# Setting up a token mixer: diagonals on VectorE, stores awaited later, first rows loaded early, a convolution moved into other tiles

## The chip, the cores and the metric

One Trainium2 chip, one of its cores. The metric is the device time of one execution in microseconds; lower is better. The kernel before was timed in three executions (5937.07, 5937.58 and 5954.27 us), of which the median, 5937.58 us, is the figure to be predicted against. One more execution was taken with the profiler.

## The reference

The program computes one layer of a decoder for a prompt of 2048 tokens and eight samples of eight tokens. The change touches two of its three token mixers, which both read the input projection `z`:

```python
z = h @ w_in
o_rw, wkv_T, shift_T = rwkv7_mix(z[..., :896], shift0, wkv0, ...)        # recurrence over tokens, 4 heads of 64
o_cv, conv_T = conformer_conv_mix(z[..., 896:1408], conv0, ...)

# rwkv7_mix:           zs = z + (z_prev - z) * mu_shift ; ... ; returns z[:, -1] as shift_T
# conformer_conv_mix:  u = z_a * sigmoid(z_b)
#                      u_pad = concat([conv0, u])               # 30 earlier rows per sequence
#                      c = causal_dwconv(u_pad, conv_w) + conv_b # 31 taps, each channel by itself
#                      return silu(layernorm(c)), u_pad[:, -30:]
```

`shift_T` (the last row of `z` of the prompt and of each sample) and `conv_T` (the last 30 rows of `u`) are outputs of the program.

## The kernel before, in words

The program runs phases one after the other: the input projection, the recurrent mixer `rwkv` with the convolution, the convolution's layer norm (`conv_finish`), attention of the prompt and of the samples, the output projection, and the gated MLP in two phases. Within a phase the five engines run their own instruction lists, written out by hand, and meet at semaphores; a `Block` ends with a barrier of all engines.

`rwkv` has two such blocks.

**The setup block** (L1204). SP issues, in this order, the loads for the convolution (weights, biases, `z`, the samples' earlier rows; `conv_inputs.sync`), the mixer's parameters (L1220, L1223), eight stores of last rows of `z` from DRAM to DRAM, four bytes a piece (`shift_p` L1225, seven times `shift_s` L1227), waits until the parameters and the eight stores have landed, then waits for ScalarE's last copy of the convolution's state, stores it (three stores, L2035 and L2036) and waits for these too (L2038). GpSimd makes masks and constants (L1246 to L1277), then the 62 diagonal matrices `cv["diag"]` (128 x 128, identity times one column of weights; two blocks of channels by 31 taps, L1281). ScalarE takes sigmoids, VectorE the products `u` into `cv["up"]` (prompt) and `cv["us"]` (samples), TensorE and ScalarE transpose the state.

**The main block** (L1283). SP loads the rows of `z` for a tile of 128 tokens into `zin` (two DMAs of 128 x 7 x 65 numbers, L1289): tile 0 on entry, tile i+1 or later when an earlier tile's shifted rows `zs` are made. TensorE first computes the samples' convolution: 62 products (block, tap) of a diagonal with `cv["us"]`, 64 columns each, into bank 4 of PSUM (L1546); it signals `conv_made`, ScalarE copies the two halves out (L1691) and signals `conv_taken`. Only then does TensorE go on to `keys_and_lora(main, 0)` and the 16 tiles of the prompt. A float32 product is two passes in the trace. Each prompt tile has 62 products of the prompt's convolution spread into places where TensorE would wait for another engine (`conv(n)` in `body`: 2, 4, 2, 6, 5, 5, 4, 4 and the rest at the end). Then follow four tiles of two samples each, whose `body` has no such products. `front` (VectorE, ScalarE) prepares the first tile: differences of rows `zd`, shifted rows `zs`, squares of keys `sqk`; ScalarE's `low_rows` needs `zs`, and TensorE's `keys_and_lora` needs `sqk` and `low_rows`. In `body` VectorE prepares the next tile's rows first (`shift`).

GpSimd has nothing to do in the main block until the prompt's last state is made.

Of the kernel before, what the change touches and what calls it, by code (L numbers as in the profile page):

```python
# [1066 lines left out]
def rwkv(nc, ident, t, cv):  # L1067
# [8 lines left out]
    with ExitStack() as ctx:  # L1076
# [123 lines left out]

        conv_made, conv_taken = [ctx.enter_context(nc.semaphore("rw_" + x)) for x in ("sample_conv_made", "sample_conv_taken")]

        setup = nc.Block()
        with ExitStack() as conv_ctx, setup:  # L1204
# [5 lines left out]
            @setup.sync  # L1210
            def _(sp):
                conv["sync"](sp)
                with nc.allow_non_contiguous_dma(reason="parameters by channel"):
                    loads = ((mu[:, :], t["mu_shift"].rearrange("(b p) -> p b", p=P)), (w0[:, :], t["w0"].partition_broadcast(P)),
                             (chp[:, 0, :], t["a0"].rearrange("(b p) -> p b", p=P)), (chp[:, 1, :], t["k_k"].rearrange("(b p) -> p b", p=P)),
                             (chp[:, 2, :], t["k_a"].rearrange("(b p) -> p b", p=P)), (ln_g[:, :], t["lnx_g"].partition_broadcast(P)),
                             (ln_b[:, :], t["lnx_b"].partition_broadcast(P)), (lora[0:32, :], t["w_lora"]), (lora[32:64, :], t["a_lora"]),
                             (lora[64:128, :], t["g_lora"]))
                    for dst, src in loads:
                        sp.dma_start(dst, src).then_inc(par, 16)  # L1220
                    sp.wait_ge(const, 1)
                    for h in range(H):
                        sp.dma_start(rk_w[64 * (h % 2):64 * (h % 2) + 64, h // 2, h:h + 1], t["r_k"][h, :].unsqueeze(1)).then_inc(par, 16)  # L1223

                    sp.dma_start(t["shift_p"].rearrange("o (b p) -> b p o", p=P), t["zT"][0:7, :, SEQ:SEQ + 1]).then_inc(shift_st, 16)  # L1225
                    for b in range(7):
                        sp.dma_start(t["shift_s"][:, b * P:(b + 1) * P].rearrange("j p -> p j"),  # L1227
                                     t["zT"][b, :, SEQ + 1:NT + 1].rearrange("p (j s) -> p j s", s=DEC_SEQ)[:, :, DEC_SEQ - 1]).then_inc(shift_st, 16)
                sp.wait_ge(par, 16 * (len(loads) + H))
                sp.wait_ge(shift_st, 16 * 8)  # L1230
                conv["sync_last"](sp)

            @setup.gpsimd
            def _(pool):
# [42 lines left out]
                own(pool.tensor_tensor(cmask[:, 1:2], sel8[:, 0:1], sel8[:, 1:2], ALU.add))  # L1277
                pool.wait_ge(conv["parameters"], 16 * 5)
                for b in range(CONV_B):
                    for j in range(CONV_W):  # L1280
                        pool.tensor_scalar(cv["diag"][:, b, j, :], ident, cv["w"][:, b, j:j + 1], None, ALU.mult)  # L1281

# [3 lines left out]
        def _(sp):  # L1286
# [6 lines left out]

            load(0)
            sp.wait_ge(*main["vec"].at("zs", 0))
# [24 lines left out]
        @block.gpsimd  # L1320
        def _(pool):
            pool.wait_ge(wkv_made, 1)
            for hp in range(2):
                pool.dma_start(t["wkv_p"].rearrange("(b two) v k -> two v b k", two=2)[hp], S_out[64 * hp:64 * hp + 64, 0, :, :]).then_inc(wkv_st, 16)
            with pool.Fori(0, S_TILES) as i:
# [6 lines left out]
                for c in range(2):  # L1332
                    pool.dma_start(t["oT"][0:2, :, bass.ds(i * 16 + (SEQ + c * DEC_SEQ), DEC_SEQ)].rearrange("b p t -> p b t"),
                                   oT_sb[:, :, c * C:c * C + DEC_SEQ]).then_inc(samp["o"].sem, 16)
            pool.wait_ge(wkv_st, 32)
            pool.wait_ge(*main["o"].at("o", TILES - 1))
# [11 lines left out]
        def _(pe):  # L1348
# [28 lines left out]

            def body(g, i, behind, ahead):
                s = g["pe"]
# [8 lines left out]

                taps = iter(() if g["sample"] else [(b, j) for b in range(CONV_B) for j in range(CONV_W)])

                def conv(n):

                    mm = None
                    for b, j in itertools.islice(taps, n):
                        mm = mul(bank(4)[:, b * P:(b + 1) * P], cv["diag"][:, b, j, :], cv["up"][:, b, bass.ds(i * P + j, P)], j == 0, j == CONV_W - 1)
                    return mm
# [143 lines left out]
                mm = conv(CONV_B * CONV_W)  # L1540
                if mm is not None:
                    mm.then_inc(*s.step("conv"))

            for b in range(CONV_B):
                for j in range(CONV_W):
                    mm = pe.matmul(bank(4)[:, b * TS:(b + 1) * TS].rearrange("p (s t) -> p s t", t=DEC_SEQ), cv["diag"][:, b, j, :], cv["us"][:, b, :, j:j + DEC_SEQ],  # L1546
                                   start=j == 0, stop=j == CONV_W - 1, skip_group_check=True)
            mm.then_inc(conv_made, 1)
            pe.wait_ge(conv_taken, 1)
            keys_and_lora(main, 0)  # L1550
# [13 lines left out]
            pe.wait_ge(*main["vec"].at("out", TILES - 1))  # L1564
            pe.wait_ge(*main["act"].at("oT", TILES - 1))
            keys_and_lora(samp, 0)
            decays(samp, 0)
            body(samp, 0, False, True)
            with pe.Fori(1, S_TILES - 1) as i:
                body(samp, i, True, True)  # L1570
            body(samp, S_TILES - 1, True, False)
            turn_out(samp, S_TILES - 1)

        @block.scalar
        def _(act):
# [112 lines left out]

            act.wait_ge(conv_made, 1)
            for b in range(CONV_B):  # L1690
                op = act.activation(cv["c"][:, b, SEQ:NT], bank(4)[:, b * TS:(b + 1) * TS], ACT.Identity, bias=cv["par"][:, 0, b:b + 1])  # L1691
            op.then_inc(conv_taken, 1)
            act.activation(warm[:, :], eps[:, :], ACT.Sigmoid)
# [302 lines left out]
def conv_inputs(nc, ident, t, cv, ps_t, ctx):  # L1996
# [15 lines left out]
    st_ld = ctx.enter_context(nc.semaphore("cv_state_loaded"))  # L2012
    stored = ctx.enter_context(nc.semaphore("cv_state_stored"))
    pe_s = Steps(nc, ctx, "cv_in_pe", ["in0", "in1", "out0", "out1", "out2"])
# [58 lines left out]

    def vector(dve):
        for b in range(CB):
            dve.wait_ge(*act_s.at(f"sig{b}", 0))
# [8 lines left out]

    return dict(sync=sync, sync_last=sync_last, gpsimd=gpsimd, tensor=tensor, scalar=scalar, vector=vector, parameters=par_ld)

# [1426 lines left out]
```

## Time and profile before

| | |
|---|---|
| median of three executions | 5937.58 us |
| the profiled execution: time | 5945.43 us |
| the profiled execution: span from first to last instruction | 5943.8 us |
| TensorE busy in the span | 4890.8 us (82%) |
| VectorE busy | 2526.8 us (43%) |
| ScalarE busy | 1904.2 us (32%) |
| GpSimd busy | 305.0 us (5%) |
| mean granted TensorE clock | 0.848 of full speed |

The profiled execution's span is within 1.7 us of its own time; that time is 7.9 us above the median of the three. In rows of a timeline the columns are: start in us, length in us of the group, engine (PE is TensorE, PEld its weight loads, DVE VectorE, ACT ScalarE, POOL GpSimd, SP SyncE, a q behind the name its queue), line, operation, what is written and read, shape, how many, and in brackets the idle time before and what ended it. In the windows view each row is a stretch, with each engine's busy us and number of instructions, then the granted clock of TensorE (1.00 is full speed), the busy share of the DMA engines and GB/s.

### The profile page before, as it was taken

The page shows a single profiled execution, that of the slowest core. Times are in us where ns is not written, and L with a number is a line of the kernel's source. Part 1 is how long each engine was busy: PE and PEld are TensorE (multiplying, and loading weights), DVE is VectorE, ACT ScalarE, POOL GpSimd, SP SyncE. Part 2 cuts the span into 40 slices and gives each one's busy share as a digit, 9 for nine tenths or more (in the row PEclk, how much of TensorE's full clock was granted, in tenths as well). Part 3 has the DMA queues.
Part 4 walks back from the last instruction along what each step waited for, and adds up shares of the span by engine and source line. Part 5 has one row for each costly group of instructions (what it writes and reads, how often), then busy time and mean ns, then how long its engine had stood idle before and what let it go on. Part 6 is the DMA issues. An engine that isn't in the chain of part 4 may idle for free. (4 is left out here: it accounts for less than half of the span.)

```text
span 5943.8 us, 68433 instructions
## 1 busy us (share of the span) xinstructions
PE 4890.8 (82%) x25340; PEld 3691.2 (62%) x25340; DVE 2526.8 (43%) x5235; ACT 1904.2 (32%) x3217; POOL 305.0 (5%) x473
## 2 busy tenths in 40 slices
PE   8999499998734566777776448888999999899999
PEld 4444388887612344545555135677888888787877
DVE  1111056765546776777861453323222222212133
ACT  1000033333326665666764432222111111101043
POOL 0000300000000000000001000010000000000000
PEclk9999589998855555666788768899999999999999
DMA  3110300000020000000002013443111111434321
GB/s 132 49 49 36 48 14 13 15 15 7 7 71 17 13 13 7 13 7 3 5 3 90 18 45 126 141 149 95 43 43 43 43 43 43 153 120 151 106 70 59
DMA packets 316997, 315.02 MB, mean 53 GB/s; under 512 B 145115, under 2 KB 266425, under 8 KB 310409
## 3 DMA queue, kind: packets, MB, share of 16 engines
q1 hardware_dynamic: 286713, 175.80, 11.0%
q0 software_dynamic: 30096, 136.76, 6.3%
q8 instruction: 112, 1.84, 0.1%
q14 instruction: 76, 0.62, 0.0%
HBM read 211.29 MB, written 102.33 MB: 53 GB/s over the span
## 5 line engine op out<-in xcount | busy, mean ns | idle before, releaser
L639 PE MATMUL fu_ps<-fu_h_hi,fu_w_lo 128*128 128x512 f32 (+1 forms) x1760 | 654.3, 372 | 34.9 <-DVE fu_h_lo L696 30.1
L640 PE MATMUL fu_ps<-fu_h_lo,fu_w_hi 128*128 128x512 f32 (+1 forms) x1760 | 653.5, 371 | 0.0
L641 PE MATMUL fu_ps<-fu_h_hi,fu_w_hi 128*128 128x512 f32 (+1 forms) x1760 | 652.2, 371 | 0.0
L2510 PE MATMUL ap_ps<-ap_V,ap_PT 128*128 128x64 f32 x2176 | 412.6, 355 | 216.7 <-ACT ap_PT L2635 216.1
L2510 PEld LDWEIGHTS ap_ps<-ap_V,ap_PT 128*128 128x128 f32 x2176 | 379.2, 263 | 270.7 <-ACT ap_PT L2635 270.6
L879 PE MATMUL fd_ps<-fd_w_lo,fd_a_hi 128*128 128x512 f32 (+1 forms) x1088 | 428.6, 394 | 21.5 <-DVE fd_w_lo L1010 18.1
L880 PE MATMUL fd_ps<-fd_w_hi,fd_a_lo 128*128 128x512 f32 (+1 forms) x1088 | 426.4, 392 | 0.0
L881 PE MATMUL fd_ps<-fd_w_hi,fd_a_hi 128*128 128x512 f32 (+1 forms) x1088 | 426.2, 392 | 0.0
L639 PEld LDWEIGHTS fu_ps<-fu_h_hi,fu_w_lo 128*128 128x128 f32 x1760 | 336.7, 191 | 93.8 <-issue 35.8
L640 PEld LDWEIGHTS fu_ps<-fu_h_lo,fu_w_hi 128*128 128x128 f32 x1760 | 336.6, 191 | 56.4
L641 PEld LDWEIGHTS fu_ps<-fu_h_hi,fu_w_hi 128*128 128x128 f32 x1760 | 336.2, 191 | 56.6
L271 PE MATMUL pi_psz<-pi_hT,pi_w 128*128 128x512 f32 (+1 forms) x880 | 341.0, 559 | 5.4 <-ACT pi_hT L236 5.4
L2531 PE MATMUL ap_ps<-ident,ap_lg 128*128 128x128 f32 x1088 | 223.9, 354 | 124.2 <-ACT ap_lg L2606 109.6
L2719 DVE TENSOR_SCALAR_CACHE_REDUCE ap_seen<-ap_sc,ap_srch 128x384 bf16<-128x384 f32 (+13 forms) x210 | 310.1, 1477 | 5.3
L2531 PEld LDWEIGHTS ap_ps<-ident,ap_lg 128*128 128x128 f32 x1088 | 174.0, 192 | 208.2 <-ACT ap_lg L2606 153.1
L2613 ACT ACTIVATE ap_sgn<-ap_sc,ap_srch 128x384 bf16<-128x384 f32 (+13 forms) x224 | 292.4, 1305 | 2.9
L672 ACT ACTIVATE fu_gpre<-fu_ps 128x512 f32<-128x512 f32 x88 | 52.5, 599 | 723.3 <-PE fu_ps L641 723.3
L271 PEld LDWEIGHTS pi_psz<-pi_hT,pi_w 128*128 128x128 f32 x880 | 171.5, 219 | 172.6 <-issue 171.7
L277 PE MATMUL pi_psz<-pi_w,pi_hT 128*128 128x512 f32 (+3 forms) x816 | 266.1, 489 | 0.0
L710 DVE TENSOR_SCALAR fu_gate<-fu_gpre,fu_cw 128x2048 f32<-128x2048 f32 x22 | 29.6, 1347 | 537.9 <-ACT fu_gprs L672 487.5
L1353 PE MATMUL rw_ps<-cv_up,cv_diag 128*128 (+1 forms) x1984 | 245.5, 276 | 0.0
L879 PEld LDWEIGHTS fd_ps<-fd_w_lo,fd_a_hi 128*128 128x128 f32 (+1 forms) x1088 | 202.5, 186 | 68.1 <-issue 18.1
(514 smaller groups left out, 8212.6 us busy)
## 6 DMA issues: line engine op xcount, KB each, us to landing
fd_x<-x SPq DMA_DIRECT2D x48, 512.0 KB, 4.6
aT<-fu_gate POOLq DMA_DIRECT2D x22, 1056.0 KB, 8.0
fu_w_raw<-in_ffn_up SPq DMA_DIRECT2D x44, 512.0 KB, 5.4
fd_a<-aT SPq DMA_DIRECT2D x32, 704.0 KB, 5.0
x<-fd_x POOLq DMA_DIRECT2D x32, 512.0 KB, 3.0
zT<-pi_zc POOLq DMA_DIRECT2D x44, 256.0 KB, 2.3
fd_w_raw<-in_ffn_down SPq DMA_DIRECT2D x10, 1024.0 KB, 11.7
za<-pi_za POOLq DMA_DIRECT2D x16, 546.0 KB, 3.2
```

What stands on the lines that cost most here:

```text
L271: mm = pe.matmul(psz[:, bank, 0:n_tok], w[:, k, c * P:(c + 1) * P], hT[:, k, 0:n_tok], start=(k == 0), stop=(k == KD - 1))
L277: mm = pe.matmul(psz[0:n, bank, 0:m], hT[:, k, s * P:s * P + n], w[:, k, N_CM + at:N_CM + at + m], start=(k == 0), stop=(k == KD - 1))
L639: pe.matmul(out, wl, hh, start=(k == 0), stop=False)
L640: pe.matmul(out, wh, hl, start=False, stop=False)
L641: mm = pe.matmul(out, wh, hh, start=False, stop=(k == KD - 1))
L879: pe.matmul(out, a_hi[:, s, k, 0:n], w_lo[:, k, cols], start=first, stop=False)
L880: pe.matmul(out, a_lo[:, s, k, 0:n], w_hi[:, k, cols], start=False, stop=False)
L881: return pe.matmul(out, a_hi[:, s, k, 0:n], w_hi[:, k, cols], start=False, stop=last)
L2510: return pe.matmul(out, lhsT, rhs, start=start, stop=stop, skip_group_check=True)
L2531: mm = pe.transpose(pb[4 + b][:, x * P:(x + 1) * P], lg[:, h, k * P:(k + 1) * P], ident)
L2613: act.activation(sgn[:, 0:keys(g)], sc[:, g % 3, 0:keys(g)], ACT.Sign, bias=state[:, NCAND:NCAND + 1], accum_out=s2[:, 0:1]).then_inc(*act ...
L2719: dve.tensor_scalar(seen[:, 0:keys(i)], row, col(CAND), 0.0, ALU.is_ge, ALU.add, accum_out=got).then_inc(*vec_s.step(f"t{i}_{r}"))
```

## The change

Five edits in `rwkv` and `conv_inputs`:

1. The 62 diagonals are made by VectorE, ahead of its products `u`, once the convolution's parameters are loaded (`conv_inputs.vector`).
2. The eight `shift` stores move from SP's setup to the start of GpSimd's list in the main block; the waits for them and for the three stores of the convolution's state move to the end of that list.
3. SP loads the first tile's rows (`first_rows`) in the setup, after the parameters, and not on entry of the main block.
4. TensorE's 62 products of the samples' convolution leave the start of the main block. The 31 of channel block 0 are spread over the first sample tile, the 31 of block 1 over the last, in the places of `conv(n)`, one fewer in each (1, 3, 1, 5, 4, 4, 3, 3, and the rest at the end; in the last tile 3 more before the rest). ScalarE copies both halves out after its last sample tile, ahead of that tile's `deviation`.
5. Before the sample tiles TensorE waits until the prompt's last convolution has been copied out of bank 4.

```diff
+        def first_rows(sp):
+            for c in range(2):
+                sp.dma_start(zin[:, c, :, :], t["zT"][0:7, :, c * C:(c + 1) * C + 1].rearrange("b p t -> p b t")).then_inc(main["z"].sem, 16)
...
-                    sp.dma_start(t["shift_p"].rearrange("o (b p) -> b p o", p=P), t["zT"][0:7, :, SEQ:SEQ + 1]).then_inc(shift_st, 16)
-                    for b in range(7):
-                        sp.dma_start(t["shift_s"][:, b * P:(b + 1) * P].rearrange("j p -> p j"),
-                                     t["zT"][b, :, SEQ + 1:NT + 1].rearrange("p (j s) -> p j s", s=DEC_SEQ)[:, :, DEC_SEQ - 1]).then_inc(shift_st, 16)
+                first_rows(sp)
+                conv["sync_last"](sp)
                 sp.wait_ge(par, 16 * (len(loads) + H))
-                sp.wait_ge(shift_st, 16 * 8)
-                conv["sync_last"](sp)
...
-                pool.wait_ge(conv["parameters"], 16 * 5)
-                for b in range(CONV_B):
-                    for j in range(CONV_W):
-                        pool.tensor_scalar(cv["diag"][:, b, j, :], ident, cv["w"][:, b, j:j + 1], None, ALU.mult)
...
-            load(0)
             sp.wait_ge(*main["vec"].at("zs", 0))
             load(P)
...
         def _(pool):
+            with nc.allow_non_contiguous_dma(reason="last rows by channel"):
+                pool.dma_start(t["shift_p"].rearrange("o (b p) -> b p o", p=P), t["zT"][0:7, :, SEQ:SEQ + 1]).then_inc(shift_st, 16)
+                for b in range(7):
+                    pool.dma_start(t["shift_s"][:, b * P:(b + 1) * P].rearrange("j p -> p j"),
+                                   t["zT"][b, :, SEQ + 1:NT + 1].rearrange("p (j s) -> p j s", s=DEC_SEQ)[:, :, DEC_SEQ - 1]).then_inc(shift_st, 16)
             pool.wait_ge(wkv_made, 1)
...
+            pool.wait_ge(shift_st, 16 * 8)
+            pool.wait_ge(conv["stored"], 16 * 3)
             pool.wait_ge(wkv_st, 32)
...
-                taps = iter(() if g["sample"] else [(b, j) for b in range(CONV_B) for j in range(CONV_W)])
+                blocks = range(CONV_B) if not g["sample"] else () if sample_taps is None else (sample_taps,)
+                taps = iter([(b, j) for b in blocks for j in range(CONV_W)])
...
+                    for b, j in itertools.islice(taps, n - 1 if g["sample"] else n):
+                        if g["sample"]:
+                            mm = pe.matmul(bank(4)[:, b * TS:(b + 1) * TS].rearrange("p (s t) -> p s t", t=DEC_SEQ), cv["diag"][:, b, j, :],
+                                           cv["us"][:, b, :, j:j + DEC_SEQ], start=j == 0, stop=j == CONV_W - 1, skip_group_check=True)
...
-            for b in range(CONV_B):
-                for j in range(CONV_W):
-                    mm = pe.matmul(bank(4)[:, b * TS:(b + 1) * TS].rearrange("p (s t) -> p s t", t=DEC_SEQ), cv["diag"][:, b, j, :], cv["us"][:, b, :, j:j + DEC_SEQ],
-                                   start=j == 0, stop=j == CONV_W - 1, skip_group_check=True)
-            mm.then_inc(conv_made, 1)
-            pe.wait_ge(conv_taken, 1)
             keys_and_lora(main, 0)
...
+            pe.wait_ge(*main["act"].at("conv", TILES - 1))
             keys_and_lora(samp, 0)
             decays(samp, 0)
-            body(samp, 0, False, True)
+            body(samp, 0, False, True, sample_taps=0)
...
-            body(samp, S_TILES - 1, True, False)
+            body(samp, S_TILES - 1, True, False, sample_taps=1)
...
-            act.wait_ge(conv_made, 1)
-            for b in range(CONV_B):
-                op = act.activation(cv["c"][:, b, SEQ:NT], bank(4)[:, b * TS:(b + 1) * TS], ACT.Identity, bias=cv["par"][:, 0, b:b + 1])
-            op.then_inc(conv_taken, 1)
...
+            act.wait_ge(conv_made, 2)
+            for b in range(CONV_B):
+                act.activation(cv["c"][:, b, SEQ:NT], bank(4)[:, b * TS:(b + 1) * TS], ACT.Identity, bias=cv["par"][:, 0, b:b + 1])
             deviation(samp, S_TILES - 1)
...
-        sp.wait_ge(stored, 16 * 3)
...
     def vector(dve):
+        dve.wait_ge(par_ld, 16 * 5)
+        for b in range(CB):
+            for j in range(CW):
+                dve.tensor_scalar(cv["diag"][:, b, j, :], ident, w[:, b, j:j + 1], None, ALU.mult)
         for b in range(CB):
             dve.wait_ge(*act_s.at(f"sig{b}", 0))
```

How the instructions stand now at two places. SP, the end of the setup and the entry of the main block, before (each row: line, operation, tiles, shape, and what it waits for; the semaphores' names are those of their first user):

```order
L1223 DMA rw_rk_w<-in_r_k 64x1 x3
L1225 DMA out_shift_p<-zT 896x1
L1227 DMA out_shift_s<-zT 128x8x1 x7
L2035 DMA out_conv_s<-cv_st_out 120x256 [waits cv_in_act,pi_w_loaded2,pi_w_loaded0]
L2035 DMA out_conv_s<-cv_st_out 120x256
L2036 DMA out_conv_p<-cv_st_out 30x256
L1204 UNCONDITIONAL_BRANCH [waits cv_state_stored,cv_parameters_loaded]
L1285 UNCONDITIONAL_BRANCH [waits barrier_Pool_Activation_PE_DVE_SP_release]
L1289 DMA rw_zin<-zT 128x7x65 x2
L1289 DMA rw_zin<-zT 128x7x65 [waits pi_vect]
```

and with the change:

```order
L1227 DMA rw_rk_w<-in_r_k 64x1 x3
L1205 DMA rw_zin<-zT 128x7x65 x2
L2038 DMA out_conv_s<-cv_st_out 120x256 [waits cv_in_act]
L2038 DMA out_conv_s<-cv_st_out 120x256
L2039 DMA out_conv_p<-cv_st_out 30x256
L1208 UNCONDITIONAL_BRANCH [waits pi_w_loaded0,cv_parameters_loaded]
L1281 UNCONDITIONAL_BRANCH [waits barrier_Pool_Activation_PE_DVE_SP_release]
L1285 DMA rw_zin<-zT 128x7x65 [waits pi_vect]
```

The eight stores of last rows are gone from SP's list, the first tile's rows stand in their place, the state's stores wait for ScalarE alone, and the branch that leaves the block waits for loads, no longer for stores.

TensorE, the first sample tile with the change (X, XT and T are the tile's own matrices; of the 31 products with `cv_us` these rows show the first 10):

```order
L1419 MATMUL rw_ps<-ident,rw_zs 128x128 x2
L1399 MATMUL rw_ps<-cv_us,cv_diag 128x64
L1355 MATMUL rw_ps<-rw_X,rw_XT 128x128 x4
L1355 MATMUL rw_ps<-rw_XT,rw_X 128x128 x4
L1399 MATMUL rw_ps<-cv_us,cv_diag 128x64 x3
L1355 MATMUL rw_ps<-rw_X,rw_X2T 128x128 x4
...
L1399 MATMUL rw_ps<-cv_us,cv_diag 128x64
...
L1355 MATMUL rw_ps<-rw_T,rw_X 128x128 x4
L1399 MATMUL rw_ps<-cv_us,cv_diag 128x64 x5
L1451 MATMUL rw_ps<-ident,rw_T 128x128 x4
```

Before, none of the rows with `cv_us` stood here; all 62 stood in one row at the head of the main block, ahead of the prompt's first `keys_and_lora`.

## Rows read from the trace of the kernel before

**Rows 1.** Windows: two stretches of setup and mixer's start, then the first tile's start.

```profile
700.00:710.00 10.00, 0.00 (x0) 0.00 (x0) 0.00 (x0) 0.00 (x0) 10.00 (x18) 0.50 0.71 1
736.60:764.30 27.70, 26.69 (x124) 26.53 (x124) 4.39 (x9) 0.04 (x1) 0.00 (x0) 0.50 0.17 35
777.00:785.00 8.00, 7.25 (x48) 6.32 (x49) 6.30 (x16) 1.68 (x3) 0.00 (x0) 0.74 0.00 0
```

**Rows 2.** Timeline of SP, 695 to 900 us: stores, then the first loads.

```profile
695.73 0.59 SPq L1225 DMA_DIRECT2D out_shift_p<-zT  x1
696.37 22.87 SPq L1227 DMA_DIRECT2D out_shift_s<-zT  x7
733.21 0.81 SPq L2035 DMA_DIRECT2D out_conv_s<-cv_st_out  x2
734.06 0.42 SPq L2036 DMA_DIRECT2D out_conv_p<-cv_st_out  x1
736.59 92.88 SPq L1289 DMA_DIRECT2D rw_zin<-zT  x8
```

**Rows 3.** Timeline: TensorE, VectorE and ScalarE at the start of the main block.

```profile
737.54 26.69 PE L1546 MATMUL rw_ps<-cv_us,cv_diag 128*128 128x64 f32 x124 [39.32 <-PEq L1204]
741.10 1.16 DVE L1733 TENSOR_TENSOR rw_zd<-rw_zin 128x448 f32<-128x448 f32 x2 [44.76 <-DMA rw_zin<-zT]
743.49 1.16 DVE L1747 TENSOR_TENSOR rw_zs<-rw_zd,rw_zin 128x448 f32<-128x448 f32 x2
764.76 0.95 ACT L1580 ACTIVATE rw_low<-rw_zs 32x128 f32<-32x128 f32 x3
766.19 1.19 PE L1353 MATMUL rw_ps<-rw_sqk,rw_headones 128*128 128x256 f32 x2 [1.97 <-ACT rw_low L1580]
777.03 1.23 PE L1353 MATMUL rw_ps<-rw_Bc,rw_RA 64*128 64x128 f32 x8 [3.85 <-DVE rw_Bc L1720]
```

**Rows 4.** One line's instructions (ns min/median/max): GpSimd's diagonals, L1281.

```profile
L1281 POOL TENSOR_SCALAR cv_diag<-ident,cv_w x62: 592/596/2721, 684.5 to 723.9; 128x128 f32<-128x128 f32 x62
```

**Rows 5.** Timeline of SP: the last convolution parameter; and line L2025's time to landing.

```profile
676.94 0.47 SPq L2025 DMA_DIRECT2D cv_par<-in_conv_ln_b  x1
...
DMA to landing us min/median/max: 2.1/2.2/4.1
```

**Rows 6.** Timeline of VectorE: a pair of like instructions; then the setup's last two groups; ScalarE's last.

```profile
744.68 0.48 DVE L1754 TENSOR_SCALAR rw_kraw<-rw_zs,rw_chp 128x128 f32<-128x128 f32 x2
...
693.32 2.28 DVE L2078 TENSOR_TENSOR cv_up<-cv_z 128x2048 f32<-128x2048 f32 x1
695.71 0.63 DVE L2083 COPY cv_tails<-cv_us 128x120 f32<-128x120 f32 x4
...
698.25 0.37 ACT L2072 ACTIVATE cv_st_out<-rw_ps 30x256 f32<-30x256 f32 x1 [0.27 <-PE rw_ps L2057]
```

**Rows 7.** Timeline: TensorE's convolution in a prompt tile; its waits in sample tiles; ScalarE at the end.

```profile
813.74 6.86 PE L1353 MATMUL rw_ps<-cv_up,cv_diag 128*128 128x128 f32 x60
1474.86 1.23 PE L1353 MATMUL rw_ps<-rw_Bc,rw_RA 64*128 64x128 f32 x8 [3.85 <-DVE rw_Bc L1720]
1493.76 0.66 PE L1444 MATMUL rw_ps<-ident,rw_T 128*128 128x128 f32 x4 [1.28 <-DVE rw_T L1720]
1503.52 1.16 PE L1353 MATMUL rw_ps<-rw_AM,rw_T 128*128 128x128 f32 x8 [0.78 <-DVE rw_T L1720]
1520.98 1.23 PE L1353 MATMUL rw_ps<-rw_Bc,rw_RA 64*128 64x128 f32 x8 [2.09 <-DVE rw_Bc L1720]
1656.54 0.66 PE L1375 MATMUL rw_ps<-ident,rw_y 128*128 128x128 f32 x2 [4.37 <-DVE rw_y L1720]
1653.59 0.30 ACT L1580 ACTIVATE rw_var<-rw_var,rw_eps 128x4 f32<-128x4 f32 x1 [1.11 <-DVE rw_var L1816]
```

**Rows 8.** Windows: a stretch of the first sample tile (columns as in rows 1).

```profile
1480.00:1485.00 5.00, 3.67 (x16) 3.47 (x16) 1.07 (x3) 1.41 (x3) 0.00 (x0) 0.57 0.00 0
```

**Rows 9.** Time to landing of the DMAs of one line, L1289 (the tile's rows).

```profile
DMA to landing us min/median/max: 3.0/3.4/4.0
```

More of the change, by code:

```diff
@@ L1199, in rwkv @@
             s.ahead = 0
-        conv_made, conv_taken = [ctx.enter_context(nc.semaphore("rw_" + x)) for x in ("sample_conv_made", "sample_conv_taken")]
+        conv_made = nc.alloc_semaphore("rw_sample_conv_made")
+        def first_rows(sp):
+            for c in range(2):
+                sp.dma_start(zin[:, c, :, :], t["zT"][0:7, :, c * C:(c + 1) * C + 1].rearrange("b p t -> p b t")).then_inc(main["z"].sem, 16)
         setup = nc.Block()
@@ L1376, in turn_out, with body @@
                 mm.then_inc(*g["pe"].step("oT"))
-            def body(g, i, behind, ahead):
+            def body(g, i, behind, ahead, sample_taps=None):
                 s = g["pe"]
@@ L1387, in each @@
                     mm.then_inc(*s.step(name))
-                taps = iter(() if g["sample"] else [(b, j) for b in range(CONV_B) for j in range(CONV_W)])
+                blocks = range(CONV_B) if not g["sample"] else () if sample_taps is None else (sample_taps,)
+                taps = iter([(b, j) for b in blocks for j in range(CONV_W)])
                 def conv(n):
                     mm = None
-                    for b, j in itertools.islice(taps, n):
-                        mm = mul(bank(4)[:, b * P:(b + 1) * P], cv["diag"][:, b, j, :], cv["up"][:, b, bass.ds(i * P + j, P)], j == 0, j == CONV_W - 1)
+                    for b, j in itertools.islice(taps, n - 1 if g["sample"] else n):
+                        if g["sample"]:
+                            mm = pe.matmul(bank(4)[:, b * TS:(b + 1) * TS].rearrange("p (s t) -> p s t", t=DEC_SEQ), cv["diag"][:, b, j, :],
+                                           cv["us"][:, b, :, j:j + DEC_SEQ], start=j == 0, stop=j == CONV_W - 1, skip_group_check=True)
+                        else:
+                            mm = mul(bank(4)[:, b * P:(b + 1) * P], cv["diag"][:, b, j, :], cv["up"][:, b, bass.ds(i * P + j, P)], j == 0, j == CONV_W - 1)
                     return mm
@@ L1540, in body @@
                 mm = conv(CONV_B * CONV_W)
-                if mm is not None:
+                if not g["sample"]:
                     mm.then_inc(*s.step("conv"))
-            for b in range(CONV_B):
-                for j in range(CONV_W):
-                    mm = pe.matmul(bank(4)[:, b * TS:(b + 1) * TS].rearrange("p (s t) -> p s t", t=DEC_SEQ), cv["diag"][:, b, j, :], cv["us"][:, b, :, j:j + DEC_SEQ],
-                                   start=j == 0, stop=j == CONV_W - 1, skip_group_check=True)
-            mm.then_inc(conv_made, 1)
-            pe.wait_ge(conv_taken, 1)
+                elif sample_taps is not None:
+                    mm.then_inc(conv_made, 1)
             keys_and_lora(main, 0)
@@ L2012, in conv_inputs @@
     st_ld = ctx.enter_context(nc.semaphore("cv_state_loaded"))
-    stored = ctx.enter_context(nc.semaphore("cv_state_stored"))
+    stored = nc.alloc_semaphore("cv_state_stored")
     pe_s = Steps(nc, ctx, "cv_in_pe", ["in0", "in1", "out0", "out1", "out2"])
@@ L2084, in vector @@
         op.then_inc(*vec_s.step("tails"))
-    return dict(sync=sync, sync_last=sync_last, gpsimd=gpsimd, tensor=tensor, scalar=scalar, vector=vector, parameters=par_ld)
+    return dict(sync=sync, sync_last=sync_last, gpsimd=gpsimd, tensor=tensor, scalar=scalar, vector=vector, stored=stored)
 def conv_finish(nc, t, cv):
```

## The prediction, made before the change was run

> **What bounds the kernel now.** The kernel is a row of phases, so I read the views in this order: first the busy shares of the page (TensorE 82%), then the windows view at the one place that the change touches, then the timelines there. In the windows [rows 1] the reader is to see a stretch of the setup in which TensorE, VectorE and ScalarE do nothing at all and only GpSimd is busy, and then one of 27.7 us in which TensorE is busy for 26.7 us while VectorE has 4.4 us of work and ScalarE none. Neither stretch is bound by the mixer's own work. The timeline of SP says who holds the setup [rows 2]: the eight four-byte stores begin at 695.73 and block SP until 733.21, when the state's stores can go out at last (ready long before: ScalarE's last copy ended at 698.62 [rows 6]); the last is issued by 734.48, and the next block's first load at 736.59. GpSimd's diagonals, from 684.5 to about 724.5 [rows 4], are shorter than that, but would hold the setup if the stores were gone. In the main block [rows 3] the tile's first work waits twice: VectorE for its rows until 741.10, then TensorE's `keys_and_lora` until 766.19, because the samples' convolution (737.54 to 764.23) stands ahead of it, and ScalarE's `low_rows` too stands behind ScalarE's copy of that convolution.
>
> The sums are against the profiled execution (5945.43 us), and what they save is then taken from the median of 5937.58 us.
>
> **Step 1, the setup's end.** Without the stores the last to finish is the chain diagonals, products `u`, tails, transposes, state's stores. The parameters have landed at 676.94 + 2.1 = 679.0 [rows 5]. A 128 x 128 instruction of VectorE: a pair takes 0.48 us, one ends 0.28 after its start, so they follow each other every 0.20 us [rows 6]; 62 x 0.20 = 12.4 us. The upper end is no overlap, 62 x 0.28 = 17.4. GpSimd still makes masks until 684.5 [rows 4]. That the two engines can hold each other up the same line shows: one of the diagonals took 2721 ns against a median of 596. If every mask excluded a diagonal, 684.5 - 679.0 = 5.5 us would be added, if none, nothing; I take half, 2.7. The diagonals then end at 679.0 + 12.4 + 2.7 = 694.1. VectorE's remaining products and tails: the second large product and the tails took from 693.32 to 696.34, 3.0 us [rows 6]; the first product 2.3 and two short ones, an estimate of 0.25 each from the pair above, make 5.8, so tails at 699.9, 3.6 later than before. ScalarE's last copy moves from 698.62 to 702.2, the three stores are issued within 1.3 us (733.21 to 734.48), and then the blocks change: 734.48 to 736.59 is 2.1 us, in which the last store also landed, so the change itself takes between nothing and 2.1, and I take 0.9. The main block starts at 704.4 in place of 736.59: **32.2 us saved**. The first rows' two loads cost SP about 0.5 us each, like its other issues in rows 2, at 696 to 697 and ahead of its wait for ScalarE, which hides them; without that cover they would cost that 1 us.
>
> The Trainium skill, "SBUF — State Buffer", section "Who interferes with whom", has a rule against this edit: GpSimd and a VectorE `tensor_scalar` in a two-port mode exclude one another for a whole instruction. By that rule in full the term is 2.8 us worse, without it 2.7 better.
>
> **Step 2, the mixer's first work.** The first rows have landed before the block starts (SP issues them at about 696 to 698, and a load lands 3.0 to 4.0 us after its issue [rows 9]). VectorE begins some 0.6 us after the start (TensorE began 0.95 after SP), `zd` to the end of `zs` takes 741.10 to 744.65, 3.6 us, and ScalarE's `low_rows` to `keys_and_lora` 764.76 to 766.19, 1.4 us [rows 3]. That is 5.6 us from block to `keys_and_lora`, at 710.0, against 766.19 - 736.59 = 29.6 us: **24.0 us saved**. From there to the tile's `body` the chain stays 777.03 - 766.19 = 10.8 us, so the body starts at 720.8.
>
> **Step 3, the samples' products in the sample tiles.** 124 passes: at full clock 6.86 / 60 = 0.114 us each, at half clock 26.69 / 124 = 0.215 [rows 3, 7]. Bounds: nothing, if all of it lies in waits, and 26.7 us, if none does. It stands in the places where TensorE waits: of the first sample tile's waits the rows show the longest within the tile (1.28 us, now five products, 5 x 0.228 = 1.14), one of the shortest (0.78, now four, 0.91) and the one after the tile's end (2.09, now seven at half clock, 3.0) [rows 7]. The last gives 0.9 us over, the middle kind 0.1 to 0.4 each; I take 1.6 for this tile. In the last tile four products at half clock (1.7) lie in a wait of 4.37, but ScalarE's two copies (764.23 to 764.76, 0.5) now stand ahead of its `deviation`, ready at 1653.59 before and then at about 1654.9: 1.3 us, with 0.8 in the tile **2.1; together 3.7 us lost**.
>
> **Step 4, the clock.** The removed products did not raise it: TensorE was busy for 26.69 of 27.7 us, and the granted clock was 0.50 of full speed, the lower level [rows 1]. It rose in the first tile at about 781.2 (the mean of 777 to 785 is 0.74), 4.2 us after the body's start; in the first sample tile, whose front is as idle as the prompt's first tile will be, at 1484.3 (the mean of 1480 to 1485 is 0.57 [rows 8]), 9.4 us after its start at 1474.86 [rows 7]. So 0 to 5.2 us more at half clock, which costs half of it at most, 2.6; I take **1.5 us lost**. The Trainium skill, "TensorE: Matmul & The Clock Gate", Part 1, says that TensorE's own activity lifts the throttle; by this the removed products were a warm-up, and this term would stand for more; the rows disagree, 0.50 to their end.
>
> **Step 5, the next tile's rows.** `load(P)` is issued when `zs` is made, at about 709, lands by 713, and is needed at about 721 when VectorE comes to `shift`. In this stretch GpSimd's eight stores run, which alone took 695.73 to 733.21, 37.5 us, on SP's queue [rows 2]. Shared evenly, the load doubles to 8 us and is in time; if it waited for all of them (704.4 + 37.5 + 3.4 = 745.3) it would cost 24. No row shows four-byte stores issued by GpSimd. I take **1.0 us lost**, nearest to the even share. GpSimd's own list waits only for the prompt's end, 700 us later, so the stores' own length, and the waits moved there, cost nothing.
>
> **Sum.** 32.2 + 24.0 - 3.7 - 1.5 - 1.0 = 50.0 us: the profiled execution would take 5895.4, the median **5887.6 us**. Edit 5, the wait for bank 4, is passed already when TensorE has waited for the tile's output, and costs nothing.
>
> **The rivals.** (A) *The samples' products are not hidden.* All 124 passes at half clock, 26.7 in place of 3.7: 27.0 saved, 5910.6. For it: the clock falls at each sample tile's end. Against it: the four waits of TensorE in rows 7 alone take 8.5 us, more than half of the 62 x 0.228 = 14.1 that all the products take at full clock. 0.10. (B) *VectorE makes the diagonals no faster than GpSimd.* 62 x 0.6 = 37.2 in place of 15.1: the setup ends 22.1 later, 27.9 saved, 5909.7. For it: the locked line above; against: VectorE's own pair at 0.20. 0.08. (C) *The clock of the first tile stays low throughout.* The tile's body ran from 777.03 to the end of its convolution at 820.60, 43.6 us [rows 3, 7], 4.2 of them at half clock; the other 39.4 at half clock are at most as much again, in place of 1.5: 12.1 saved, 5925.5. Against it: the sample tile's rise after 9.4 us. 0.05. (D) *GpSimd's stores hold the rows back*, the one that ends slower: if the stores take T on its queue, and the tile's load waits for all of them, the loss is 704.4 + T + 3.4 - 721, or T - 13. From T = 64 on, 1.7 times what SP needed, the change loses; at four times (150 us) 137 is lost in place of 1.0, and the time is 6023.6. For it: no row shows such a store on that queue. Against it: the queue has no other work, and the load is on SP's. 0.03. Two of A to C together, near 5930: 0.04. That leaves 0.70 for the forecast.
>
> **Range and chances.** The best case takes the kind end of each bound: 2.7 for the masks, 3.7, 1.5 and 1.0, so 58.9 saved, 5878.7. The likeliest case's bad end adds 5.0 (no overlap on VectorE), 2.8 (masks), 1.2 (blocks), 10 (a load that waits for part of the stores), 5 (products), 1.1 (clock): 24.9 saved, 5912.7. A and B lie inside. With some 4 us of scatter at either end: 5874 to 5916, which leaves out C, D and the pair, 0.12, and a little of the forecast's own. A measurement of this kernel tells a change from none at about 0.3%, 17.8 us: faster means below 5919.8. The forecast, A and B are there: 0.88; C and the pair give 0.09 for the same; D gives 0.03 for slower.
>
> **What would show it.** Right: SP's first load of the main block's second tile at about 709; VectorE's 62 diagonals of 0.20 us apiece from 679; `keys_and_lora` at about 710; no row of TensorE between the setup's transposes and that; the sample tiles about 2 us longer each. Wrong: VectorE's first `shift` in tile 0 waiting on a DMA (step 5, D); diagonals slower than 0.28 (B); the clock at 0.50 beyond 731 (C); a gap at the end of the first sample tile well above 1 us (A).

## The result, and the profile after

The changed kernel took 5908.0 us (median of four executions, 5904.2 to 5911.2); the kernel before, run beside it on the same chip, 5945.9 (5937.1 to 5954.3). The ratio is 0.9936, with a 95% interval of 0.9915 to 0.9957: faster by some 38 us. The forecast was 5888 (5874 to 5916): right in direction and inside its range, but 20 us too low. Some 8 of the 20 come from the kernel before, whose median was 5937.6 when the forecast was made and is 5945.9 with a fourth execution. The other 12, a gain of 38 us in place of 50, are not scatter: one step of the sum failed. The profiled execution took 5909.1 us with a span of 5907.5 (clock 0.851).

The two traces, each counted from the setup's first instruction of ScalarE (671.04 before, 668.83 after; these 2.2 us come from the input projection, not from the change):

| from the setup's start to | before, us | after, us | saved so far |
|---|---|---|---|
| VectorE's first `zd` | 70.1 | 31.3 | 38.8 |
| `keys_and_lora` of tile 0 | 95.2 | 36.3 | 58.9 |
| the body of tile 0 | 106.0 | 47.1 | 58.9 |
| tile 0's last convolution products | 142.7 | 106.9 | **35.8** |
| the body of the first sample tile | 803.8 | 767.8 | 36.0 |
| the last copy to `oT` of the last sample tile | 986.2 | 952.9 | 33.3 |

The gain was there, more than forecast, and 23 us of it went within the first tile. The timelines of SP, GpSimd, VectorE and TensorE there, which answer to [rows 2, 3, 4]:

```profile
676.85 12.92 DVE L2080 TENSOR_SCALAR cv_diag<-ident,cv_w 128x128 f32<-128x128 f32 x62 [18.41 <-DMA cv_par<-in_conv_ln_b]
693.26 1.19 SPq L1205 DMA_DIRECT2D rw_zin<-zT  x2
697.69 0.82 SPq L2038 DMA_DIRECT2D out_conv_s<-cv_st_out  x2
699.98 0.80 POOL L1318 DMA_DIRECT2D out_shift_p<-zT  x1 [16.75 <-POOLq L1208]
700.08 1.16 DVE L1736 TENSOR_TENSOR rw_zd<-rw_zin 128x448 f32<-128x448 f32 x2 [4.70 <-PEq L1208]
700.77 6.10 POOL L1320 DMA_DIRECT2D out_shift_s<-zT  x7
703.65 45.83 SPq L1285 DMA_DIRECT2D rw_zin<-zT  x4
705.11 1.19 PE L1355 MATMUL rw_ps<-rw_sqk,rw_headones 128*128 128x256 f32 x2 [7.85 <-ACT rw_low L1584]
715.95 1.23 PE L1355 MATMUL rw_ps<-rw_Bc,rw_RA 64*128 64x128 f32 x8 [3.86 <-DVE rw_Bc L1723]
738.30 1.16 DVE L1736 TENSOR_TENSOR rw_zd<-rw_zin 128x448 f32<-128x448 f32 x2 [21.83 <-DMA rw_zin<-zT]
742.12 2.05 PE L1355 MATMUL rw_ps<-rw_X,rw_XT 128*128 128x128 f32 x8 [20.84 <-DVE rw_XT L1861]
775.72 6.86 PE L1355 MATMUL rw_ps<-cv_up,cv_diag 128*128 128x128 f32 x60
```

The reader is to see 62 diagonals in 12.9 us, the state's stores 33 us earlier (28.9 us from the setup's start in place of 62.2), and then, at 738.30, a wait of 21.83 us: VectorE comes to the second tile's `shift`, and its rows, issued at 703.65, are not there. TensorE stands behind it for 20.84 us. The DMA view of 699 to 740 us says what those rows ran beside (a queue's row: packets, MB, share of the 16 engines' time; an issue's: how many, KB each, median us from issue to landing):

```profile
q0 software_dynamic: 256, 0.03, 55.8%
q1 hardware_dynamic: 2046, 0.65, 13.9%
...
rw_zin<-zT SPq DMA_DIRECT2D x2, 227.5 KB, 31.8
out_shift_s<-zT POOLq DMA_DIRECT2D x7, 4.0 KB, 24.6
```

The load's two halves landed after 29.4 and 34.2 us in place of 3.4 [rows 9], while GpSimd's queue took over half of the engines' time with its eight stores. An estimate from these rows: one of its packets held an engine for 1.4 us on average (0.558 x 41 x 16 / 256), one of SP's for 0.04. GpSimd's stores go out every 0.87 us from 700.77 on, so five of the eight are ahead of the load and three behind it. The wait has a second effect, in the windows view (columns as in rows 1): TensorE's clock had risen shortly after 720, fell back to 0.50 while TensorE stood still, and was at 0.99 again only from 748 on.

```profile
720.00:730.00 10.00, 1.28 (x8) 1.09 (x6) 0.00 (x0) 1.08 (x2) 0.00 (x0) 0.67 0.79 20
730.00:740.00 10.00, 0.00 (x0) 0.00 (x0) 1.67 (x3) 0.00 (x0) 0.00 (x0) 0.50 0.23 23
748.00:752.00 4.00, 4.00 (x38) 4.00 (x37) 2.09 (x5) 1.71 (x5) 0.00 (x0) 0.99 0.58 119
```

The sample tiles, which answer to [rows 7]:

```profile
1477.58 3.09 PE L1399 MATMUL rw_ps<-cv_us,cv_diag 128*128 128x64 f32 x14
1480.60 1.23 PE L1355 MATMUL rw_ps<-rw_Bc,rw_RA 64*128 64x128 f32 x8
1615.77 1.97 PE L1399 MATMUL rw_ps<-cv_us,cv_diag 128*128 128x64 f32 x8 [0.37 <-ACT rw_S_out L1584]
1617.78 0.52 ACT L1713 ACTIVATE cv_c<-rw_ps,cv_par 128x64 f32<-128x64 f32 x2 [2.06 <-PE rw_ps L1399]
```

From body to body the first sample tile took 44.0 us, against 46.1 before, and the seven products at its end fill the wait that stood there, with no gap behind. The last one, from its body to its last copy (1621.77), took 46.9 against 43.0; there four products and ScalarE's copies stand alone at the end. Neither difference is the products' alone, as the windows of the two tiles say (columns as in rows 1; two rows each before, after, and of e6_diag, an experiment below whose sample tiles are those of the changed kernel):

```profile
1474.86:1520.98 46.12, 34.76 (x307) 29.16 (x307) 23.62 (x62) 14.01 (x31) 2.40 (x4) 0.80 0.06 7
1614.25:1657.23 42.98, 29.45 (x296) 24.99 (x296) 24.44 (x60) 8.54 (x20) 3.86 (x6) 0.86 0.02 4
1436.61:1480.60 43.99, 39.51 (x368) 35.15 (x368) 24.20 (x63) 14.32 (x32) 2.40 (x4) 0.89 0.07 8
1574.87:1621.77 46.90, 39.09 (x358) 35.28 (x358) 24.42 (x60) 8.95 (x23) 3.86 (x6) 0.79 0.02 4
1439.27:1485.09 45.82, 41.48 (x369) 37.07 (x369) 24.23 (x63) 14.32 (x32) 2.40 (x4) 0.84 0.07 8
1578.35:1623.01 44.66, 36.69 (x358) 32.88 (x358) 24.43 (x60) 8.95 (x22) 3.86 (x6) 0.84 0.02 5
```

The granted clock of the first tile was 0.89 in place of 0.80, that of the last 0.79 in place of 0.86: the first was shorter with 62 passes more because more of it ran at the higher level. The products did not bring that about: with them the clock rose 4.4 us after the tile's body here and 9.2 in e12_behind, without them 9.4 before the change and 5.0 in e5_back. Over all traces with these products the first tile took 43.5 to 45.9 us.

### The profile page after: what moved, and what is told of

Same layout as the page of the kernel before. It is cut to its first block and busy times, and to the rows that moved or that the text cites. A ratio compares the mean times of both kernels' runs of the same rounds, so it can differ in the third digit from the quotient of the medians.

```text
span 5907.5 us, 68437 instructions
## 1 busy us (share of the span) xinstructions
PE 4880.7 (83%) x25340; PEld 3686.3 (62%) x25340; DVE 2538.8 (43%) x5297; ACT 1904.7 (32%) x3217; POOL 272.9 (5%) x419
```

## The experiments

Each changes the changed kernel, or a run that it names, in one point. The first question was the load.

**e1_spread.** No store under way together with a load:

```diff
+                pool.wait_ge(*main["z"].at("z", 1))
                 pool.dma_start(t["shift_p"].rearrange("o (b p) -> b p o", p=P), t["zT"][0:7, :, SEQ:SEQ + 1]).then_inc(shift_st, 16)
                 for b in range(7):
+                    pool.wait_ge(*main["z"].at("z", 2 + b))
```

> GpSimd sends the eight four-byte stores one per tile, each when the rows of tile 1, 2, ... 8 have landed, so that none is under way with a load. Theory (the DMA engines take packets of GpSimd's queue and of SP's in turn, and a store's packets are so much longer that a load beside them ends only with them): tile 1's rows land 3 to 4 us after their issue in place of 34.2, VectorE's 21.83 us wait in tile 0 is gone, tile 0 from its body to its last convolution is back at about 37 us (36.7 before the change, 59.8 after), and the time is about 5885 us. Rival (the slow load has another cause, such as the place at which it is issued): the load stays at 34 us and the time at 5908.

Measured: 5885.4 us (5883.3 to 5891.2), 0.9925 of before [0.9912 to 0.9939]. The DMA view of 702.5 to 706 us, then the timelines:

```profile
rw_zin<-zT SPq DMA_DIRECT2D x2, 227.5 KB, 3.4
```

```profile
716.16 1.23 PE L1357 MATMUL rw_ps<-rw_Bc,rw_RA 64*128 64x128 f32 x8 [3.86 <-DVE rw_Bc L1725]
716.60 1.16 DVE L1738 TENSOR_TENSOR rw_zd<-rw_zin 128x448 f32<-128x448 f32 x2
753.17 6.86 PE L1357 MATMUL rw_ps<-cv_up,cv_diag 128*128 128x128 f32 x60
```

VectorE's `zd` has no wait, and the tile takes 37.0 us from body to last convolution (36.7 before the change, 59.8 after). The stores beside the load are the cause.

**e2_three.** `for b in range(3)` in place of 7, and the wait at the end for four stores.

> Leaves out four of the seven shift_s stores (those rows of the output are not written), the rest as in the change. Theory: the stores' packets halve (4 of 8 stores), their end and with it the load's comes at about 719 instead of 738 on the changed kernel's time line, some 15 to 16 us after its issue, and VectorE's wait in tile 0 falls from 21.8 to about 2.5 us. Rival (a fixed price for starting GpSimd's queue beside SP's): the load stays near 34 us and the wait near 22.

```profile
725.66 1.16 DVE L1736 TENSOR_TENSOR rw_zd<-rw_zin 128x448 f32<-128x448 f32 x2 [9.13 <-DMA rw_zin<-zT]
```

The load landed after 20.2 and 21.5 us, the wait was 9.1 (a single execution, 5891.6 us). So the wait goes with the stores and is no fixed price of the queue. That more was left than was expected of half of them fits the order of the issues: of the five stores ahead of the load this run keeps four. One store alone lands after 8.1 us (e1_spread), and four took to about 724, so the length is no plain multiple.

**e3_act.** The eight issues moved from GpSimd's list to the head of ScalarE's, `pool.` turned into `act.`.

> ScalarE instead of GpSimd sends the eight stores, at the same place, the main block's start. On SP's queue in the kernel before, the same stores went as one packet per element (8390 packets, 37.5 us), on GpSimd's as 256. Theory (packets in turn): the load's 112 packets per DMA engine each wait for one four-byte packet of 37.5 us / 504 = 0.074 us, so it lands after about 3.4 + 8.3 = 12 us, before it is needed (13 us): VectorE's wait in tile 0 is 0 to 2 us, and the time is near 5886. Rival (four-byte stores fill the DMA engines, whoever sends them): the load takes over 30 us and VectorE waits about 20.

The timeline of ScalarE, then the DMA view of 702.5 to 706 us, and of 699 to 745 us the row of ScalarE's queue:

```profile
702.04 28.21 ACTq L1580 DMA_DIRECT2D out_shift_s<-zT  x7
730.41 0.95 ACT L1584 ACTIVATE rw_low<-rw_zs 32x128 f32<-32x128 f32 x3
```

```profile
rw_zin<-zT SPq DMA_DIRECT2D x2, 227.5 KB, 21.9
...
q10 hardware_dynamic: 8192, 0.03, 15.2%
```

Neither: the load's halves took 19.3 and 24.6 us, twice the theory's 12, though every store packet here is one element and all of them together took 15.2% of the engines' time over these 46 us. So neither long packets nor full engines are needed for a slow load. That no wait for rows shows is only because ScalarE, which needs 28 us to issue the stores, has `low_rows` queued behind them and brings the whole tile 27 us late (a single execution, 5917.6 us).

**e4_behind.** The same issues on SP, behind `load(P)`:

```diff
             sp.wait_ge(*main["vec"].at("zs", 0))
             load(P)
+            with nc.allow_non_contiguous_dma(reason="last rows by channel"):
+                sp.dma_start(t["shift_p"].rearrange("o (b p) -> b p o", p=P), t["zT"][0:7, :, SEQ:SEQ + 1]).then_inc(shift_st, 16)
...
```

> SP sends the eight stores itself, right behind the second tile's load, so on one queue with it. Theory (turns are between queues, and one queue is in order): this load lands in 3 to 4 us, the stores by about 746, the third tile's load behind them near 750, before it is needed: no wait of VectorE for rows over 2 us in tiles 0 to 2, time near 5885. Rival (stores fill the engines whoever sends them): the load takes over 20 us, with a wait of over 10.

A single execution of 5878.4 us, and no wait for rows: `zd` of the second tile starts at 715.84. The same program with another last tile (e8_best) shows that load landing after 3.3 us.

**e7_late.** All eight on GpSimd, with the first of e1_spread's two waits alone.

> The changed kernel with one wait: GpSimd sends all eight stores in a row, but only when the second tile's rows have landed. Theory (a load beside the stores is slow, and that costs only where it has no slack): the second tile's load takes 3 to 4 us and VectorE's 21.8 us wait is gone; the third tile's load, issued about 727 while the stores run until about 744, takes 15 to 22 us, and is needed only 31 us after its issue, so no wait; time near 5885. Rival (the stores hold up the tiles' own work too, wherever they run): a wait of over 5 us in tile 0 or 1, and a time over 5892.

A single execution of 5886.2 us; no wait for rows. The second tile's load took 3.0 and 3.5 us, the third tile's 18.3 and 20.1, hidden by its slack of about 31. The same slow load costs 22 us in one place and nothing in the next.

**e9_after_load.** The eight stores behind `pool.wait_ge(*main["vec"].at("zs", 0))`, to separate turns between queues from order of arrival.

> The changed kernel with one wait: GpSimd starts its eight stores when zs of tile 0 is made, the event at which SP issues the second tile's load, so the load stands some 1 us ahead of the first store instead of behind four of them. Theory (the engines take the two queues' packets in turn, whichever was issued first): a load whose 112 packets per engine are under way when the stores come is still drawn out to 15 to 35 us, with a wait of VectorE of 5 us or more in tile 0. Rival (order of arrival: a load waits only for the stores issued ahead of it): it lands 3.5 to 6 us after its issue, no wait, time near 5886.

The DMA view of each half of the load, issued at 704.1 and 704.6 us, and what moved from 703 to 745 us in 40 slices of 1.05 us:

```profile
rw_zin<-zT SPq DMA_DIRECT2D x1, 227.5 KB, 3.2
...
rw_zin<-zT SPq DMA_DIRECT2D x1, 227.5 KB, 11.9
```

```profile
GB/s 0 0 141 259 55 0 1 2 1 1 0 0 1 0 0 2 2 1 1 1 2 1 2 16 15 20 13 25 24 25 28 28 25 42 38 155 28 0 0 0
```

A single execution of 5889.2 us, no wait: mostly the rival. The half issued ahead of the first store (704.39) was unhurt; the other, 0.2 us behind it, landed at 716.5, just in time. The third to fifth slices hold (141 + 259 + 55) x 1.05 = 478 KB, the whole load (455 KB): its bytes had moved by 708.2, and its completion came 8 us later, when stores were landing (the first at 713.9). The Trainium skill, "DMA: Bandwidth & Descriptors", "Queues, rings and completion order", says that a DMA's semaphore write lands only after every earlier write of its DMA engine, across queues; this row agrees. The same section of the Trainium skill says that an engine takes turns between queues by packets. That alone does not give the sizes: e3_act's load, beside one-element packets, should then have landed after about 12 us.

**e10_two.** Only `shift_p` and one `shift_s` ahead of the load, six from `zs` on (a wait at `b == 1`).

> The changed kernel, but GpSimd sends only shift_p and the first shift_s before the second tile's load, and the other six when zs of tile 0 is made, at the load's own issue. Theory formed from the runs so far (order of arrival, whichever queue: a load lands 0 to 6 us after the stores issued ahead of it have landed): shift_p and the first shift_s land at about 718 (16.9 us after the latter's issue at 700.8), so the load lands at 718 to 724 and VectorE waits 1.5 to 7 us in tile 0; time near 5890. Rival (packets in turn until all stores are through): the load lands near 738 and VectorE waits about 20 us; time near 5907.

```profile
726.62 1.16 DVE L1738 TENSOR_TENSOR rw_zd<-rw_zin 128x448 f32<-128x448 f32 x2 [10.61 <-DMA rw_zin<-zT]
```

Between the two (a single execution, 5893.4 us): the halves landed after 14.8 us, at 718.0, as expected, and after 23.0, at 726.6, which was not. But GpSimd's third store went out at 703.45, ahead of the second half, and landed at 722.8, so this half too came within 4 us of the last store ahead of it; the last store of all landed only at 737.9. A load does not wait for all stores. Counted from the landing of the last store that was issued ahead of it, each half of the load read there came between 1.1 us before and 4.6 us after in e2_three, e3_act, e7_late, e9_after_load and here. The changed kernel is the exception, and so is e11_after, the same kernel again: five stores ahead, the fifth landed at 728.0 (727.5), the halves at 733.0 and 738.3 (732.6 and 737.9), 5 and 10 us later. What makes it later there, the three stores behind or something else, is not shown: e9_after_load and e10_two have stores behind too.

The other questions are what the moved parts are worth.

**e5_back.** On e1_spread, the samples' products and ScalarE's copy stand at the main block's head again, as the lines that the change removed.

> e1_spread with the samples' products and ScalarE's copy of them put back at the head of the main block, as they stood before the change; all else as in e1_spread. Theory (the products cost there what they take, and are nearly hidden in the sample tiles): keys_and_lora comes 28 us after the block's start in place of 5, 23 us later; the last sample tile and the convolution's finish give back about 5 us, the first sample tile takes 2 more; the clock rises in tile 0 about as long after its body as in e1_spread. About 5885 + 20 = 5905 us. Rival (the products at the head warm the clock, or the sample tiles pay for them in full): within 5 us of e1_spread's 5885.

```profile
700.98 26.69 PE L1557 MATMUL rw_ps<-cv_us,cv_diag 128*128 128x64 f32 x124 [3.17 <-PEq L1208]
740.48 1.23 PE L1357 MATMUL rw_ps<-rw_Bc,rw_RA 64*128 64x128 f32 x8 [3.86 <-DVE rw_Bc L1732]
```

```profile
700.00:727.00 27.00, 26.02 (x122) 26.05 (x123) 4.39 (x9) 0.00 (x0) 0.80 (x1) 0.50 0.10 21
742.00:746.00 4.00, 3.71 (x20) 2.81 (x16) 3.93 (x11) 0.69 (x2) 0.00 (x0) 0.61 0.00 0
```

5913.2 us, 0.9965 [0.9955 to 0.9976]. From the setup's start the body of tile 0 comes after 71.3 us against 47.1 in e1_spread, 24.1 later, and the last sample tile's last copy 22.6 later, so 1.5 came back: 1.2 of it are the four sample tiles (44.3 against 45.0 for the first, 140.3 against 140.8 for the rest), a difference within what the clock moves in these tiles. The 62 products cost 24 at the head and little in the sample tiles. They warm nothing: the clock rose at about 745, 4.6 us after the body, and in e1_spread, without them, 4.8 after (718 to 722 us has a mean of 0.63).

**e6_diag.** On e1_spread, the diagonals on GpSimd behind its masks again.

> e1_spread with the 62 diagonals made by GpSimd after its masks, as before the change. Theory (diagonals on GpSimd hold the setup once the stores are gone): they run from about 684 to 723, the main block starts 22 to 25 us later than in e1_spread, the time is 5907 to 5910 us. Rival (the setup's end hangs on the products, tails and state's stores, and the diagonals are off the path on either engine): the block starts within 3 us of e1_spread's, time about 5887.

The costliest group of GpSimd from 668 to 725 us (busy us and mean ns behind the bar), and VectorE's first instruction of the main block:

```profile
L1281 POOL TENSOR_SCALAR cv_diag<-ident,cv_w 128x128 f32<-128x128 f32 x62 | 40.1, 668 | 0.1
```

```profile
723.79 1.16 DVE L1742 TENSOR_TENSOR rw_zd<-rw_zin 128x448 f32<-128x448 f32 x2 [29.08 <-PEq L1208]
```

5908.3 us, 0.9964 [0.9950 to 0.9977]. The block starts 23.1 us later than in e1_spread (54.4 against 31.3 from the setup's start). With the stores gone from the setup, the diagonals are its end if GpSimd makes them.

**e8_best.** e4_behind, with `n` in place of `n - 1` products at each place of the last sample tile.

> The stores on SP behind the second tile's load (e4_behind), and in the last sample tile each place takes one product more, so that all 31 lie inside it and none stands behind its last state. Theory: the second tile's rows land in 3 to 4 us; the last sample tile, 46.2 us in the changed kernel, is 1 to 3 us shorter; the time is 5880 to 5885 us, at least as good as e1_spread's 5885. Rival (the products cost the same wherever they stand in a tile at half clock): the last tile stays at 46 us.

5887.9 us (5882.3 to 5890.2), 0.9926 [0.9913 to 0.9940]. The last tile took 42.8 us from its body to its last copy, against 46.9 in e1_spread (and in the changed kernel, not the 46.2 of the expectation). How much of the 4 us is the placing is not shown: the granted clock of the tile was 0.90 against 0.79, and in e6_diag, with the old placing and 0.84, it took 44.7. The whole program's time is no better than e1_spread's, nor than that of e4_behind (5878.4, and 5880.5 in e12_behind).

**e11_after and e12_behind**, the changed kernel and e4_behind again, on one chip.

> The changed kernel itself once more, so that it stands on the same chip as the run beside it. Both theories: its profile shows the second tile's load at some 34 us and VectorE's wait of about 22 us in tile 0 again; ratio to before near 0.9936.

> e4_behind once more, timed on the same chip as the changed kernel: the stores on SP behind the second tile's load. Theory (the wait in tile 0 is lost time): 20 to 24 us under e11_after's median. Rival (much of the wait is given back later in the program): under 10 us.

5901.3 us (5899.1 to 5906.9), 0.9950 [0.9936 to 0.9963], with a wait of 21.1 us for the rows; and 5880.5 (5868.5 to 5889.4), 0.9912 [0.9896 to 0.9928]. The difference is 20.9 us, and the intervals do not meet: the wait is lost time, and the kernel with the stores on SP is faster than the changed kernel and than the one before. SP's and VectorE's timelines of e12_behind:

```profile
703.31 1.01 SPq L1285 DMA_DIRECT2D rw_zin<-zT  x2
704.37 0.61 SPq L1293 DMA_DIRECT2D out_shift_p<-zT  x1
705.01 19.53 SPq L1295 DMA_DIRECT2D out_shift_s<-zT  x7
724.98 42.88 SPq L1285 DMA_DIRECT2D rw_zin<-zT  x4
716.05 1.15 DVE L1736 TENSOR_TENSOR rw_zd<-rw_zin 128x448 f32<-128x448 f32 x2
```

SP is held by its own stores for 20 us, but nothing is queued behind them that is due before 724.98.

## Why the prediction was right, and where it was not

**Steps 1 and 2 held.** Together they were to save 56.2 us and saved 58.9. The surplus is in step 1, the setup's end: 15.1 us were put for the diagonals, 2.7 of them for the masks' lock, and the 62 took 12.9. The lock is there, but small: the diagonals while GpSimd's masks ran (until 683.2) and after, in ns as in rows 4, then a group of six masks beside the diagonals and the same group before the change:

```profile
L2080 DVE TENSOR_SCALAR cv_diag<-ident,cv_w x29: 273/277/473, 676.8 to 683.0; 128x128 f32<-128x128 f32 x29
L2080 DVE TENSOR_SCALAR cv_diag<-ident,cv_w x33: 270/273/275, 683.2 to 689.5; 128x128 f32<-128x128 f32 x33
677.57 2.48 POOL L1246 TENSOR_SCALAR_AFFINE_SELECT rw_tri<-rw_tri 128x128 f32<-128x128 f32 x6
679.72 2.10 POOL L1246 TENSOR_SCALAR_AFFINE_SELECT rw_tri<-rw_tri 128x128 f32<-128x128 f32 x6
```

A diagonal followed the last every 0.22 us in the first stretch and every 0.20 in the second, some 0.6 us in all, and the six masks took 0.4 us longer. The Trainium skill's rule of exclusion ("SBUF — State Buffer", "Who interferes with whom"), for which the prediction had 5.5 us in full, shows itself here with no more than that. The parameters landed where they were put, and step 2's 24.0 came out at 23.9. Diagonals on GpSimd, which start behind its masks, cost 23.1 us in e6_diag, near the 22.1 of rival B, whose diagonals were as slow, but on VectorE.

**Step 3 was right in kind and too dear**, as far as the clock lets it be told. The four sample tiles of the changed kernel lost 2.8 us in place of 3.7 (2.1 gained in the first, 1.0 lost in the third, 3.9 in the last), but the granted clock moved in them too. The nearest comparison is e6_diag, whose two middle tiles took 46.7 and 46.5 us as before the change: its first tile gained 0.3, its last lost 1.7, against 1.6 and 2.1 put down as losses. The products lie in the waits, as argued from rows 7, and the last tile is the worse one, as was said. Rival A's 26.7 for products that are not hidden was 24 at the head of the block.

**Step 4 was right in kind.** The removed products were no warm-up. Alone, in e1_spread, the term is 0.3 us (37.0 against 36.7) in place of 1.5; in the changed kernel the wait for rows let the clock fall again.

**Step 5 failed.** "Shared evenly, the load doubles to 8 us and is in time": it took 34.2, and the tile gave back 23 us where 1.0 was allowed. The bad end of 24, which the same step worked out and set aside, was the truth. The step was mis-sized in two ways. It took the even share from nothing: the only row for such stores, 37.5 us on SP's queue, spoke of their own length, and no row spoke of a share. And it took the range's bad end at 10 us of this loss, though 24 had been worked out. Rival D had the mechanism right, and its formula too: on GpSimd's queue the stores took 38.1 us (699.98 to 738.1), about as long as on SP's, so T - 13 is 25, near the 23.1 measured. What did not come was a T of 64 or more, with which D begins to decide.

**That the time still lies in the range is luck.** Step 5 overran its own bad end by some 11 us (a wait of 21.8 against 1.0 and 10 more), and only because the other bad ends, 15.1 us for VectorE, masks, blocks, products and clock, stayed all but unused did the sum end inside.

Put together from the setup's start: 58.9 saved by the first tile's body, 23.1 given back in it, 2.5 lost from its end to the last copy. That is 33.3. Another 1.4 went between the mixer's last store and the convolution's finish; e5_back has the same gap (6.05 us against 4.67 before), so the products are not its cause, and it was not followed further. The other 4.4 of the 36.3 us between the two spans lie ahead of the setup (2.2) and behind the finish's start (2.2), where nothing was changed.

**Open:** why a load beside these stores is slow by so much. That the stores are the cause is shown; of the mechanism, that a load lands about when the stores issued ahead of it do, on GpSimd's queue and on ScalarE's, that in the changed kernel it came later still, and that completions can lag the bytes. Whether the DMA engines or the memory's small writes set the pace was not tried.

## What to carry to other kernels

A transfer that nobody waits for still has a price: ask which load with little slack runs beside it, and whether it could instead be issued on that load's own queue, behind it. When a step has two ends worked out and no row between them, keep the bad one in the range whole. Before a few us between two tiles are put down to an edit, compare their granted clock. A wait removed from the setup is worth what the next-longest chain leaves, so both parts, here stores and diagonals, have to go together.

## What was not expected of the hardware

Eight DMAs of 4 KB or less, four bytes an element, drew out a load of 455 KB from 3.4 to 34.2 us, though they are 0.03 MB. The same elements were 8390 packets on SP's queue (with a few others, 695.5 to 734 us before) and 256 on GpSimd's, and took about as long. Issuing them cost GpSimd 0.87 us each, ScalarE 2.6 (median, 9.9 at most) and SP 2.8 (19.53 / 7). And a load whose bytes had all moved could complete 8 us later (e9_after_load).
